# Three pairs of steps in five feed-forward stages computed as seven block products, with four sums of weight blocks on VectorE

## The reference, cut to what matters

```
D_MODEL = 1024
SEQ = 256
D_FF = 2816

def swiglu(h, w_gu, w_down):
    gate, up = jnp.split(h @ w_gu, 2, axis=-1)
    return (jax.nn.silu(gate) * up) @ w_down

def swiglu_2(x, w_gate, w_up, w_down):
    return (jax.nn.silu(x @ w_gate) * (x @ w_up)) @ w_down

def macaron_ffn(xs, g, shift, scale, gate, w_gate, w_up, w_down):
    return xs + 0.5 * gate * swiglu_2(modulate(xs, g, shift, scale), w_gate, w_up, w_down)
```

## Time and profile before

| | |
|---|---|
| median of three runs | 3576.23 us (3574.46 to 3582.94) |
| span of the profiled execution, first to last instruction | 3574.0 us |
| TensorE (PE) busy | 3487.5 us, 98% of the span, 18564 matmuls |
| weight loads of TensorE (PEld) busy | 2960.8 us, 83% |
| VectorE (DVE) busy | 2211.7 us, 62% |
| ScalarE (ACT) busy | 1712.6 us, 48% |
| DMA | 654.63 MB, mean 183 GB/s |
| mean granted TensorE clock | 0.997 |

### The profile page before, as it was taken

How to read it: one execution, slowest core, us unless ns; L and a number is a source line. 1 busy time by engine, 2 the same in 40 slices (tenths; PEclk the granted TensorE clock), 3 DMA queues, 4 the chain that set the end, 5 groups by cost and what they waited for, 6 DMA issues and landing times. The chain is left out here.

```text
span 3574.0 us, 45127 instructions
## 1 busy us (share of the span) xinstructions
PE 3487.5 (98%) x18564; PEld 2960.8 (83%) x18564; DVE 2211.7 (62%) x2603; ACT 1712.6 (48%) x2073; POOL 113.8 (3%) x116
## 2 busy tenths in 40 slices
PE   9999999999999998999999999999999999999999
PEld 7889888888888887888889878888888678888887
DVE  5776656676667677576677555555556555545655
ACT  5454454544645446545454354545453454545543
POOL 0001100000000000000001100000000000000000
PEclk9999999999999999999999999999999999999999
DMA  7642156664476763676742145555554135454453
GB/s 271 239 154 79 60 202 234 216 231 176 156 271 252 258 226 123 224 282 227 280 178 93 60 177 189 182 184 183 183 175 154 60 142 189 172 189 164 156 209 130
DMA packets 90554, 654.63 MB, mean 183 GB/s; under 512 B 10096, under 2 KB 10224, under 8 KB 11632
## 3 DMA queue, kind: packets, MB, share of 16 engines
q1 hardware_dynamic: 79344, 574.15, 44.2%
q0 software_dynamic: 11008, 77.60, 6.0%
HBM read 650.66 MB, written 1.05 MB: 182 GB/s over the span
## 5 line engine op out<-in xcount | busy, mean ns | idle before, releaser
L2013 DVE TENSOR_TENSOR w_lo<-raw,w_hi 128x2048 fp32r<-128x2048 f32 x540 | 1234.2, 2290 | 614.5 <-ACT w_hi L1382 614.3
L1382 ACT ACTIVATE w_hi<-raw 128x2048 fp32r<-128x2048 f32 (+1 forms) x542 | 1032.7, 1909 | 499.2 <-PE acc L584 401.1
L582 PE MATMUL wrk<-w_hi,h_hi 128*128 128x512 f32 (+1 forms) x2400 | 939.6, 391 | 15.8 <-issue 5.4
L584 PE MATMUL wrk<-w_hi,h_lo 128*128 128x512 f32 (+1 forms) x2400 | 923.9, 385 | 0.0
L583 PE MATMUL wrk<-w_lo,h_hi 128*128 128x512 f32 (+1 forms) x2400 | 922.4, 384 | 0.0
L582 PEld LDWEIGHTS wrk<-w_hi,h_hi 128*128 128x128 f32 x2400 | 451.5, 188 | 105.2 <-issue 14.2
L584 PEld LDWEIGHTS wrk<-w_hi,h_lo 128*128 128x128 f32 x2400 | 451.3, 188 | 91.4
L583 PEld LDWEIGHTS wrk<-w_lo,h_hi 128*128 128x128 f32 x2400 | 452.1, 188 | 84.1 <-issue 0.2
L582 PE MATMUL acc<-w_hi,hid_hi 128*128 128x512 f32 (+1 forms) x1160 | 452.8, 390 | 4.6 <-DVE hid_lo L2115 4.5
L584 PE MATMUL acc<-w_hi,hid_lo 128*128 128x512 f32 (+1 forms) x1160 | 450.0, 388 | 0.0
L583 PE MATMUL acc<-w_lo,hid_hi 128*128 128x512 f32 (+1 forms) x1160 | 449.6, 388 | 0.0
(11 more groups left out here) (298 smaller groups left out, 4005.5 us busy)
## 6 DMA issues: line engine op xcount, KB each, us to landing
raw<-in_wts SPq DMA_DIRECT2D x541, 1024.0 KB, 4.8
arena<-in_mods POOLq DMA_DIRECT2D x72, 1024.0 KB, 5.1
const<-in_const SPq DMA_DIRECT2D x1, 2112.0 KB, 17.1
c<-in_bias POOLq DMA_DIRECT2D x8, 256.0 KB, 3.0
x<-in_x SPq DMA_DIRECT2D x2, 512.0 KB, 6.5
c<-in_c SPq DMA_DIRECT2D x1, 1024.0 KB, 4.8
out<-x SPq DMA_DIRECT2D x2, 512.0 KB, 2.6
row<-in_rows SPq DMA_DIRECT2D x1, 512.0 KB, 17.8
```

The costliest lines, as they stand in the source:

```text
L582: nc.tensor.matmul(o, l_h, r_h, start=first, stop=False, skip_group_check=True)
L584: return nc.tensor.matmul(o, l_l, r_h, start=False, stop=last, skip_group_check=True)
L1382: return nc.scalar.activation(o, i, f, **kw)
L2013: tt(w_lo[:, ns % SLOTS, :], raw[:, ns % SLOTS, :], w_hi[:, ns % SLOTS, :].bitcast(F32), ALU.subtract).then_inc(lo_ready, 1)
```

## The change

In the last five feed-forward stages (`b0_ctx`, `b0_ffn0`, `b0_ffn1`, `b1_ffn0`, `b1_ffn1`) the steps 2 and 3, 5 and 6, 8 and 9 are computed as pairs; the steps 0, 1, 4, 7 and 10 stay as they were. A pair's gate and up product is (2 token halves x 2 input halves) by (2 input halves x 512 columns of gate and 512 of up): eight block products of 12 matmuls before. It is now the scheme of seven products, with sums of blocks on both sides. With A the input (A11 to A22, `shifted`) and B the weight blocks (B11 and B21 for gate, B12 and B22 for up), the seven products, each 12 matmuls with a split of its own, are in the program's names B11, B21, T2, T3, T1, T4, B22.

- **Weights:** the four blocks B11, B12, B22, B21 of a pair are loaded into `arena` (not into `raw`), and VectorE makes four sums of 128x2048 from them: T1 = B11 + B12 and T2 = T1 + B22 and T3 = B12 + B22 in the single step before the pair, T4 = B21 + T2 amid the pair (signs are taken care of on the input's side and when the weights are laid out). In the first pair of a stage T3 is made inside the pair instead. The ring of splits gets 7 entries for a pair instead of 4.
- **Input:** once per stage VectorE makes four sums of 128x512 (`factors`, L2533 to L2536 after), ScalarE and VectorE their hi and lo parts `x_hi` and `x_lo` (L2541).
- **Results:** bank A of a pair collects B11, T2, T3, T4 one after the other; ScalarE copies it out after each of the first three (`part`), TensorE waits for that copy before the next one; after T4 it takes silu of it. VectorE adds and subtracts the parts (L2589, L2595, L2602) and multiplies (L2600, L2604).
- **Order:** the down product of the single step before a pair is run between T2 and T3. The two down products of a pair follow in the single step behind it.
- The statistics of the following stage move from step 4 to 7, those of `final_norm` from step 2 to 4, the gate rows from step 6 to 10. `rstd` shares the memory of `row`, and the scratch of GpSimd's DMAs is set to 2048.

The core of the diff:

```
+PAIRS = {n: (2, 5, 8) for n in ("b0_ctx", "b0_ffn0", "b0_ffn1", "b1_ffn0", "b1_ffn1")}
...
+def ring_items(name):
+    items, owed = [], []
+    for unit in units(name):
+        kind, s = unit
+        if kind == "one":
+            items += [("g", s, 0), ("g", s, 1)] + [("d", q) for q in owed]
+        else:
+            items += [(b, s) for b in ("B11", "B21", "T2")] + [("d", owed[0])] + [(b, s) for b in ("T3", "T1", "T4", "B22")]
+            items += [("d", q) for q in owed[1:]]
+        owed = steps_of(unit)
+    return items + [("d", q) for q in owed]
...
+HOME = dict(B11=0, B12=1, B22=2, B21=3, T1=4, T3=1, T2=0, T4=3)
+HELD_BY = dict(B11="T4", B12="T3", B22="B22", B21="T4")
...
 SP:
+                    if s == firsts[0]:
+                        sp.wait_ge(x_new, before(i, "x"))
...
+                    else:
+                        sp.wait_ge(lo_ready, ring_at[i, (HELD_BY[name], firsts[firsts.index(s) - 1])] + 1)
+                    sp.dma_start(blocks[HOME[name]], wts[k]).then_inc(block_landed[HOME[name]], 16)
...
 TensorE:
+                def pair(s, owed):
...
+                    plain("B11", s, a, 0, 0, True)
+                    b = bank(use[name, f"B{s}"])
+                    plain("B21", s, b, 4, 0, True)
+                    for q in owed:
+                        turn_hid(q)
+                    pe.wait_ge(part_out, 3 * g + 1)
+                    summed("T2", s, a, False)
+                    down_all(owed[0])
+                    pe.wait_ge(part_out, 3 * g + 2)
+                    summed("T3", s, a, False)
+                    o = bank(use[name, f"C{s}"])
+                    summed("T1", s, o, True)
+                    pe.wait_ge(part_out, 3 * g + 3)
+                    plain("T4", s, a, 4, 1, False)
+                    pe.wait_ge(up_second, g + 1)
+                    summed("B22", s, o, False)
...
 ScalarE:
+                def pair(s, owed):
...
+                    split_to(n + 2)
+                    part("B11", s, part_a)
+                    split_to(n + 3)
+                    for q in owed:
+                        hid_high(q)
+                    split_to(n + 4)
+                    part("T2", s, part_b)
+                    split_to(n + 5)
+                    act.wait_ge(gate_first, g + 1)
+                    fn(part_d, part_d, ACT.Silu).then_inc(e_ready, 1)
+                    split_to(n + 7)
+                    part("T3", s, part_c)
+                    split_to(n + 8)
+                    act.wait_ge(w_used, at("T4", s) + 1)
+                    fn(part_a, wrk[:, use[name, f"A{s}"] % BANKS, :], ACT.Silu).then_inc(e_ready, 1)
...
 VectorE:
+                    split_to(n + 3)
+                    for q in owed:
+                        hid_low(q)
+                    if s == PAIRS[name][0]:
+                        add_blocks("T3", s)
+                    split_to(n + 4)
...
+                    tt(part_d, bank_of("B"), part_a, ALU.add).then_inc(gate_first, 1)
+                    split_to(n + 5)
+                    add_blocks("T4", s)
+                    split_to(n + 7)
...
+                    tt(part_e, bank_of("C"), part_c, ALU.subtract).then_inc(up_second, 1)
+                    split_to(n + 8)
```

More of the change, by code:

```diff
@@ L288, in build @@
 def build(nc, wts, vec_d, const_d, x_d, c_d, bias_d, mods_d, rows_d, out, ops):
-    starts, use, total = schedule(ops)
+    starts, use, ring, loads, total = schedule(ops)
+    ring_at = {(i, item): starts[i]["ns"] + n for i, (kind, name, _) in enumerate(ops) if kind == "ffn" for n, item in enumerate(ring_items(name))}
+    users = {what[1]: n for n, what in enumerate(ring) if what[0] == "raw"}
     with ExitStack() as ctx:
@@ L443, in before @@
                 return sum(k == "ffn" for k, _, _ in ops[:i])
+            if what == "paired":
+                return sum(n in PAIRS for _, n, _ in ops[:i])
             if what == "x":
@@ L545, in _ @@
             first_c = [i for i, o in enumerate(ops) if o[2].get("x") == "c"][0]
-            ahead = starts[op_at("ffn2_3")]["ns"] + SLOTS
+            ahead = starts[op_at("ffn2_3")]["loads"] + SLOTS
             load_all(0, 1)
@@ L554, in _ @@
             sp.dma_start(c[:], c_d[:]).then_inc(c_loaded, 16)
-            end = starts[len(ops) - 2]["ns"] + 6
+            sp.dma_start(row[:], rows_d[:, 0, :]).then_inc(row_loaded, 16)
+            end = starts[len(ops) - 2]["loads"] + 6
             load_all(ahead, end)
@@ L1527, in ffn @@
                     split_to(ns + 3 * s + 3)
[L1528 to L1531, removed]
                     if name in AHEAD and s == AHEAD_AT:
@@ L2010, in lo @@
             def lo(ns):
+                what, k = ring[ns]
+                v = raw[:, k % SLOTS, :] if what == "raw" else blocks[HOME[what]]
                 dve.wait_ge(hi_ready, ns + 1)
-                tt(w_lo[:, ns % SLOTS, :], raw[:, ns % SLOTS, :], w_hi[:, ns % SLOTS, :].bitcast(F32),
+                tt(w_lo[:, ns % SLOTS, :], v, w_hi[:, ns % SLOTS, :].bitcast(F32),
                    ALU.subtract).then_inc(lo_ready, 1)
@@ L2948, in ffn_pieces, with block @@
     d = down.reshape(STEPS, 2, P, D).transpose(0, 2, 1, 3).reshape(STEPS, P, PW)
-    order = [g[0]]
-    for s in range(1, STEPS):
-        order += [g[s], d[s - 1:s]]
-    return order + [d[STEPS - 1:]]
+    def block(which, s):
+        w, half = (gate, up)[int(which[2]) - 1], int(which[1]) - 1
+        v = w.reshape(2, 4, P, F)[half, :, :, 256 * s:256 * s + NB]
+        return v.transpose(1, 0, 2).reshape(P, PW)
+    order = []
+    for item in load_items(name):
+        order.append(g[item[1], item[2]] if item[0] == "g" else d[item[1]] if item[0] == "d" else block(*item))
+    return [np.stack(order)]
 def out_pieces(w):
```

467 lines of the change are left out of this document (422 added, 45 removed).

## The result

| | before | after |
|---|---|---|
| median of 13 runs each | 3577.84 us (3574.05 to 3582.94) | 3585.88 us (3581.45 to 3592.36) |
| span of the profiled execution | 3574.0 us | 3590.5 us |
| mean granted TensorE clock in it | 0.997 | 0.992 |

The ratio is 1.0024, with a 95% interval of 1.0016 to 1.0032: 8 us slower by the medians.

The account below looks back on a forecast made before the run. TensorE, busy for 98% of the span, was taken as the bound. The span of 3574.0 us, less 1.6 (walk), plus 4.5 (clock), gives 3576.9; with 2.2 from span to median, 3579.1 us, range 3564 to 3598.

Parts of the forecast that it names:

- 15 pairs, 12 matmuls less in each: TensorE's matmuls removed from the pairs, all on the path: 15 x 2.72 = 40.8 us saved.
- later pair, stop in front of T4: In ten later pairs TensorE waits 0.7 us for T4's split, 0.8 with restart; net 1.9 us saved each.
- first pair, stops at B21 and T4: In five first pairs TensorE waits 1.2 us for B21 and 3.8 for T4; 5.3 late with restarts, net 2.6 lost.
- starts: Input sums delay step 1's split at five stage starts: 0.4 us in three, 1.1 in two, together 3.4 us.
- final_norm: Its statistics, moved into the step before b0_ctx's second pair, cost 1 us, between 0 and 2.6.
- clock in the five stages: The 3.8 us pause in first pairs lowers TensorE's clock in three of five, at 1.5 us each: 4.5 us.
- The walk: Step-by-step timing of engines through pairs, with starts and final_norm: -19 + 13 + 3.4 + 1 = -1.6 us.
- the rival of all five falls: The clock falls after the long pause in all five first pairs, 1.75 us each: 3583.4 us; chance 0.15.
- A lower clock only after these five: Expected sign: TensorE's clock is lowered only behind the long pauses of the five first pairs.
- all of it is hidden: Rival: VectorE's added work never stops TensorE in the pairs, T4 split in time everywhere: 3540 us; chance 0.04.
- VectorE as the bound: Rival: VectorE needs over 47.6 us a cycle, 0.4 us more per large instruction; no chance of its own.
- every pair like the first: Rival: VectorE leaves the single step late, so all pairs stall; 45 us plus 9 of clock, 3632; chance 0.09.

Follow-up runs that it names:

- experiment 2: Changed kernel plus seven unused plain matmuls on TensorE in front of T4 in the five first pairs; 3580.6 us, ratio 1.0009.
- Experiment 4: Changed kernel with the x products reading columns of h_hi and h_lo instead of x_hi and x_lo (results not the reference's); 3587.8 us, one run.
- experiments 3: Changed kernel with only steps 2 and 3 of each of the five stages paired, the other steps single as before; 3611.2 us, ratio 1.0095.
- experiment 1: Changed kernel with the sum T4 moved on VectorE ahead of the splits of T3 and T1 in all 15 pairs; 3556.1 us, ratio 0.9939.
- experiment 5: Kernel of experiment 1 with x_hi and x_lo placed before row in SBUF, each starting at a multiple of 8 KB; 3550.75 us, ratio 0.9920.

## Why the prediction was right, and where it was off

The forecast was 3579.1 us, 2.9 us above the median it started from, in a range of 3564 to 3598, with "the same" as the likeliest class. Measured: 3585.9, 8.0 us or 0.24% above before. The range is 34 us wide, so that it held says little; what the runs bear out is the mechanism, term by term:

| term | predicted, us | measured, us |
|---|---|---|
| 15 pairs, 12 matmuls less in each | -40.8 | -40.8 |
| later pair, stop in front of T4 | 10 x 0.8 = 8 | 10 x 0.57 = 5.7 |
| first pair, stops at B21 and T4 | 5 x 5.3 = 26.5 | 5 x 5.15 = 25.8 |
| starts | 3.4 | 3 x 0.4 + 1.9 = 3.1 |
| final_norm | 1 | 1.0 |
| pitch of the x products | none | 720 x 0.006 = 4.3 |
| clock in the five stages | 3 x 1.5 = 4.5 | some 9 |
| sum | 2.6 | 8.1 |

A stop is measured as what lies between the starts of the matmuls around it, less a pace, and the first matmul's own delay behind it: at T4 of the first pair 3449.28 - 3445.41 - 0.23 = 3.64, and 0.1 more. The clock's 9 us are what the five stages of the profiled execution have more than those of experiment 2. As a check by another way, the five stages of the three profiles of after are 7.7, 9.2 and 10.0 us longer than before's (942.9 us).

- *The walk* held to a few tenths of a microsecond, and the sum takes 2.29 us, as the row of the same size said. In experiment 2, which has no fall in these stages, the last three of them are 0.56, 0.66 and 0.37 us shorter than before; the terms give 0.6. b0_ffn0 is 0.4 us longer, where the terms give no change, b0_ctx 1 or 2 us more than they give, and what these are stays open.
- *The later pair.* The stop of 0.8 us is 0.57 (0.33 us of it shown as idle, where 0.6 was forecast). That is no error in VectorE's line: TensorE comes 0.22 us later, being held up by the slower x matmuls ahead. Experiment 4 takes that away; its stop is 0.57 us of idle time, 0.81 us by the starts, as forecast.
- *The clock.* The mechanism was right, the frequency too low: "a fall to the lower level in three of five, at 1.5 us". In three profiles of after and in experiments 3 and 4, 23 of 25 pauses of 3.42 to 3.55 us had a fall behind them. A fall costs 1.6 us; 4 of the 14 in after kept the clock low for longer, and b1_ffn0 is another 1.2 us longer with such a one (193.2 against 192.1 us in two profiles of after). By its mechanism the nearest of the cases was the rival of all five falls, 3583.4, to which the forecast gave a chance of 0.15. This is the term that was mis-sized: 4.5 us for what measured 9 in the profiled execution.
- *"A lower clock only after these five"* was wrong: b0_attn had falls as well, though no kernel can be named as their cause.
- *The term that was missing* is the pitch: I took one pace for all matmuls of 512 columns, and 720 of them are slower by 6 ns, 4.3 us. Most of that is hidden, though: TensorE comes later to T4 and stands less in front of it, which is why the later and the first pairs were given too much (2.3 and 0.7 us). What it adds is some 1 us, in line with the little that experiment 4 gained. So nearly all of the 5.1 us by which the forecast of the change was short is the clock: 4.5 + 4.3 - 2.3 - 0.7 - 0.3 (starts) = 5.5.
- *The rivals.* That all of it is hidden was refused for a line of 14.7 us that has 14.05. That line isn't a bound of VectorE but an order: experiment 1 runs the same instructions without the wait, at 3556 us; what then still lies above that rival's 3540 is B21 (7 us), the pitch (4.3) and a median of before that is 1.6 us above the one the forecast started from; some 3 us stay open. VectorE as the bound, and every pair like the first, did not occur.
- *Two slips without effect.* The window 10:15 from which a fall was priced begins 2.1 us before the pause ends; the 1.7 us lost are the same. And 3579.1 + 45 + 9 is 3633, not 3632.

## What to carry to other kernels

When two engines in turn prepare an operand, look at the idle time of both: here each waited for the other for 2 to 4 us while TensorE stood, and moving one sum ahead of two splits that nobody yet needed was worth 30 us, three to four times the 8 us by which the change had made the kernel slower. A pause of TensorE of 3.4 us, in a kernel like this one, is to be counted with its fall of the clock, 1.6 us or more (23 of 25 had one). And the pace of a matmul is to be read, or looked for afterwards, for each operand by itself.

## What the hardware showed

- **The place of a stationary operand sets the pace.** Matmuls of 512 columns whose weights come from `x_hi` or `x_lo` start 0.2335 us apart while these stand behind tensors such as `vec` (805 columns, 3220 bytes), and 0.228 us apart when they stand at multiples of 8 KB (experiment 5). Which boundary matters wasn't tried.
- **GpSimd and VectorE take turns when each reads two SBUF sources.** GpSimd's sum that began at 3367.16 beside a split took 3.23 instead of 1.30 us, and ended 1.16 us after that split (3369.23); two splits that began beside a sum took 5.61 instead of 4.49 us. The Trainium skill ("SBUF — State Buffer", section "SBUF: two separate sides") describes an exclusive lock, held for the whole instruction, on which the other engine blocks. The trace agrees: each loses about what the other had left.
- **At middling pauses the fall of the clock is a matter of the execution.** The pauses of 1.2 to 2.6 us in b0_attn had one fall among them in one execution of the changed kernel and five in another, 246.1 against 250.5 us for the same stage. Behind 3.42 to 3.55 us 23 of 25 pauses had one.
